# Key sums of the stick-breaking attention: fp32 operands replaced by a high and a low part, split by ScalarE and GpSimd

## The reference

```
z = jnp.einsum('bthd,bhsd->bhts', qb, kh).astype(jnp.float32) * scale
past = s_pos[None, :] < t_pos[:, None]
log_1m = jnp.where(past, jax.nn.log_sigmoid(-z), 0.0)
tail = lax.cumsum(log_1m, axis=3, reverse=True) - log_1m
w = jnp.where(past, jnp.exp(jax.nn.log_sigmoid(z) + tail), 0.0)
return jnp.einsum('bhts,bhsd->bthd', w.astype(v.dtype), vh)
```

## Time and profile before

| | us |
|---|---|
| median of 3 runs (1684.21 to 1684.86) | 1684.85 |
| the profiled execution, its own time | 1684.58 |
| its span, first to last instruction | 1682.5 |
| PE busy | 1669.5 (99%) |
| DVE busy | 1229.0 (73%) |
| ACT busy | 861.7 (51%) |
| POOL busy | 107.3 (6%) |

### The profile page before, as it was taken

How to read it: one execution, slowest core, us unless ns; L and a number is a source line. 1 busy time by engine, 2 the same in 40 slices (tenths; PEclk the granted TensorE clock), 3 DMA queues, 4 the chain that set the end, 5 groups by cost and what they waited for, 6 DMA issues and landing times.

```text
span 1682.5 us, 24105 instructions
## 1 busy us (share of the span) xinstructions
PE 1669.5 (99%) x9040; PEld 1405.3 (84%) x9040; DVE 1229.0 (73%) x1841; ACT 861.7 (51%) x1108; POOL 107.3 (6%) x141
## 2 busy tenths in 40 slices
PE   8999999999999999999999999999999999999999
PEld 6888887788888888878778888888888787788887
DVE  6777847776777676779876767776767798767675
ACT  6444556644445444566564444444445665644442
POOL 2000100200002000101011000030001010100000
PEclk9999999999999999999999999999999999999999
DMA  7645443465547555534444555475554344446552
GB/s 280 230 175 201 152 160 126 163 225 182 192 175 242 197 193 189 166 123 149 128 163 167 219 183 191 175 236 206 190 192 164 121 149 130 163 166 217 186 189 75
DMA packets 69812, 299.95 MB, mean 178 GB/s; under 512 B 5408, under 2 KB 7680, under 8 KB 44512
## 3 DMA queue, kind: packets, MB, share of 16 engines
q1 hardware_dynamic: 66752, 291.52, 49.3%
q0 software_dynamic: 2688, 7.19, 1.6%
q10 hardware_dynamic: 288, 0.10, 0.0%
HBM read 297.74 MB, written 1.05 MB: 178 GB/s over the span
## 4 chain that ended last, share of the span: by engine, by line
PE 98%; DVE 1%; ACT 1%; DMA 0%; issue 0%; POOL 0%; ACTq 0%
PE ps L590 26%; PE ps L601 14%; PE ps L643 9%; PE ps L644 9%; PE ps L645 9%; PE ps L878 6%; PE ps L880 6%; PE ps L879 6%; PE ps L565 2%; PE ps L566 2%; PE ps L968 1%; PE ps L568 1%; PE ps L366 1%; PE ps L572 1%; PE ps L1049 1%; PE ps L1021 1%
## 5 line engine op out<-in xcount | busy, mean ns | idle before, releaser
L273 DVE TENSOR_TENSOR w_lo<-raw,w_hi 128x2048 fp32r<-128x2048 f32 x275 | 627.3, 2293 | 141.6 <-ACT w_hi L266 140.8
L266 ACT ACTIVATE w_hi<-raw 128x2048 fp32r<-128x2048 f32 x275 | 524.2, 1912 | 254.5 <-PE ps L601 166.2
L590 PE MATMUL ps<-aT,w_hi 128*128 128x512 f32 x1920 | 489.9, 392 | 0.0
L590 PEld LDWEIGHTS ps<-aT,w_hi 128*128 128x128 f32 x1920 | 344.2, 188 | 59.5
L601 PEld LDWEIGHTS ps<-aT,w_lo 128*128 128x128 f32 x1920 | 270.4, 190 | 25.1
L601 PE MATMUL ps<-aT,w_lo 128*128 128x256 f32 x1920 | 277.2, 282 | 0.0
L791 DVE TENSOR_REDUCE tmp<-ps 128x256 f32<-128x512 f32 x240 | 164.7, 686 | 131.9 <-PE ps L601 131.7
L643 PE MATMUL ps<-w_hi,act_hi 128*128 128x512 f32 x576 | 226.1, 393 | 0.8 <-ACT gate_or_gain L913 0.8
L644 PE MATMUL ps<-w_lo,act_hi 128*128 128x512 f32 x576 | 224.9, 390 | 0.0
L645 PE MATMUL ps<-w_hi,act_lo 128*128 128x512 f32 x576 | 224.2, 389 | 0.0
L878 PE MATMUL ps<-w_hi,aT 128*128 128x512 f32 (+1 forms) x432 | 171.6, 397 | 0.0
(11 more groups left out here) (303 smaller groups left out, 1561.6 us busy)
## 6 DMA issues: line engine op xcount, KB each, us to landing
raw<-in_ffn_units SPq DMA_DIRECT2D x197, 1024.0 KB, 5.0
raw<-in_w_in SPq DMA_DIRECT2D x34, 1024.0 KB, 5.3
raw<-in_w_gate SPq DMA_DIRECT2D x24, 1024.0 KB, 5.1
raw<-in_w_out SPq DMA_DIRECT2D x12, 1024.0 KB, 4.8
qk_t<-in_nsa_cmp_w POOLq DMA_DIRECT2D x8, 512.0 KB, 5.8
raw<-in_w_br_b SPq DMA_DIRECT2D x4, 1024.0 KB, 4.8
raw<-in_w_br_a SPq DMA_DIRECT2D x2, 1024.0 KB, 4.9
raw<-in_w_br_c SPq DMA_DIRECT2D x2, 1024.0 KB, 4.9
```

The lines of the kernel that those rows point to most:

```text
L266: nc.scalar.activation(w_hi[w][:, :], raw[k][:, :], ACT.Copy).then_inc(hi_ready, 1)
L273: nc.vector.tensor_tensor(w_lo[w][:, :], raw[k][:, :], w_hi[w][:, :].bitcast(F32), ALU.subtract)\
L590: nc.tensor.matmul(gu_bank(like, j), hi[:, k, GU_COLS[j]:GU_COLS[j] + P], aT[:, :, a, :], start=a == 0, stop=a == KC - 1, skip_group_check ...
```

## The change

In both large mixers the sums over the keys take four one-pass products for two plain fp32 products. ScalarE writes `hi`, a copy of the logarithms in type F32R (`act_sb_split`), and GpSimd writes `lo = pt_buf - hi` (`pool_sb_split`). Half 0 goes into the first 768 columns of `oT_hi` and `oT_lo`, half 1 into `act_hi` and `act_lo`. The two constant matrices are copied once in each mixer into the last 256 columns of `oT_lo`, by ScalarE (`sums_neg`). TensorE waits for `sb_sp_lo`, which GpSimd counts, where it waited for `sb_sp_ready`. The two quarters of tile (5, 0) now stand ahead of the two halves of the sums, one each. On VectorE `ahead(9)` moves behind the compressed keys.

```diff
+        def sb_split(half, h):
+            if half == 0:
+                return [o[:, 3 * P * h:3 * P * (h + 1)] for o in oT_flat]
+            return [a[:, 0:3 * P] for a in act_flat[h]]
+        def act_sb_split(act, half, li):
+            act.wait_ge(sem("sb_sp_ready"), 2 * li + half + 1)
+            for h in range(2):
+                last = nc.scalar.activation(sb_split(half, h)[0], sb_view(ptb, half)[:, h, :], ACT.Copy)
+            last.then_inc(sem("sb_sp_hi"), 1)
+        def pool_sb_split(pool, half, li):
+            pool.wait_ge(sem("sb_sp_hi"), 2 * li + half + 1)
+            for h in range(2):
+                hi, lo = sb_split(half, h)
+                last = nc.gpsimd.tensor_tensor(lo, sb_view(ptb, half)[:, h, :], hi.bitcast(F32), ALU.subtract)
+            last.then_inc(sem("sb_sp_lo"), 1)
...
-                add(0, 3 * P, const("tail_neg"), own)
-                add(P, S, const("ones_neg"), own[:, S:3 * P])
+                for own in sb_split(half, h % 2):
+                    add(0, 3 * P, tail, own)
+                for own in sb_split(half, h % 2):
+                    add(P, S, ones, own[:, S:3 * P])
...
                 if i == 0:
+                    for half_ in range(2):
+                        pool_sb_split(pool, half_, ph["mix2_before"])
                     wait(pool, "kc_ss_ready", ph)
...
             for half_ in range(2):
-                pe.wait_ge(sem("sb_sp_ready"), 2 * li + half_ + 1)
+                quarter(5, 0, half_)
+                pe.wait_ge(sem("sb_sp_lo"), 2 * li + half_ + 1)
                 pe_sb_logw(pe, half_, ph)
-            tile(5, 0)
             tile(5, 1)
...
             ahead(7)
+            nc.scalar.activation(sums_neg, consts[:, place["ones_neg"][0]:place["ones_neg"][0] + 2 * P], ACT.Copy)
             evac(3, 0)
...
+            act_sb_split(act, 0, li)
             evac(4, 0)
             ahead(9)
+            act_sb_split(act, 1, li)
             evac(4, 1)
...
                 last.then_inc(sem("sb_sp_ready"), 1)
-            ahead(9)
             wait(dve, "kcvc_ready", ph)
...
+            ahead(9)
             qk_normed(0, qk_first, "qk_first_ready")
```

More of the change, by code:

```diff
@@ L1796, in pe_sb_scores @@
             last.then_inc(ev("sb_z_ready", ph)[0], 1)
+        oT_flat = [o[:, :, :].rearrange("p a b -> p (a b)") for o in (oT_hi, oT_lo)]
+        act_flat = [[a[:, :, :].rearrange("p a b -> p (a b)") for a in pair] for pair in zip(act_hi, act_lo)]
+        sums_neg = oT_flat[1][:, 6 * P:8 * P]
+        def sb_split(half, h):
[13 more added lines that the diff above has]
+            last.then_inc(sem("sb_sp_lo"), 1)
         def pe_sb_logw(pe, half, ph):
-            sp_ = sb_view(ptb, half)
+            tail, ones = sums_neg[:, P:2 * P], sums_neg[:, 0:P]
             for h in (2 * half, 2 * half + 1):
-                dst, own = sb_bank(h), sp_[:, h % 2, :]
+                dst = sb_bank(h)
                 def add(c0, c1, a, b):
                     return nc.tensor.matmul(dst[:, c0:c1], a, b, start=False, stop=True, skip_group_check=True)
-                add(0, 3 * P, const("tail_neg"), own)
-                add(P, S, const("ones_neg"), own[:, S:3 * P])
+                for own in sb_split(half, h % 2):
+                    add(0, 3 * P, tail, own)
+                for own in sb_split(half, h % 2):
+                    add(P, S, ones, own[:, S:3 * P])
                 add(0, P, ident_bf, notpast_bf)
```

## The result

| | us |
|---|---|
| before, median of 16 runs | 1684.40 (1684.13 to 1686.10) |
| after, median of 16 runs | 1688.82 (1686.91 to 1689.20) |
| ratio | 1.0023, 95% interval 1.0016 to 1.0030 |
| the profiled execution after, its own time | 1687.26 |

The change made the kernel 4.4 us slower, 0.26%, just over the 0.2% named as the least that a measurement tells. The runs of after fall into two groups: four from 1686.91 to 1687.48, at a mean granted clock of 0.999, and twelve from 1688.50 to 1689.20, at 0.998 but for one. The profiled execution is one of the four.

A forecast was written before the change was run, and what follows sets the result against it. TensorE, busy 1669.5 of 1682.5 us, bounds the kernel. A mixer saves 1.3 and waits 2.5, +1.2; two mixers +2.4 give 1687.0 for the profiled execution, 1687.2 as median, 8-in-10 range 1681.8 to 1689.8.

The forecast's parts named there:

- The saving: TensorE's sums over the keys: a head takes 0.69 us, saving 1.3 us a mixer, bounds 0.75 and 1.7.
- The port: GpSimd and VectorE instructions with two SBUF operands take turns at a shared port, the waiting engine next; GpSimd's subtraction 1.0 us.
- The wait: TensorE before half 1 of the sums waits for GpSimd's fourth subtraction, 2.5 us a mixer; bounds 2.0 and 3.7.
- Who stands behind: Later users of VectorE: normalization 3.0 us late, 1.6 us slack at the attention's weights; 0.2 at most, left out.
- rival A: Wait at the sums hidden, GpSimd beside VectorE or keeping the port: 1682.2 us, 1681.4 to 1683.4; 22%.
- The clock: Granted clock in idle stretches: a fall would add to rival B; 1.00 in the first 5 us speaks against; unsized.
- rival B: Longer wait at the sums, 3.7 us or more, VectorE also late for the attention: 1689.6 to 1692 us; 14%.
- The moved `ahead(9)`: On VectorE behind the compressed keys: free where its unit is used, but puts 2.29 us of port between GpSimd's instructions.
- rival C: Short wait at the sums, about as long as the saving: 0 to +0.7 us a mixer, 1684.9 to 1686; 12%.
- Rival D: One-pass products of the sums cost as much as fp32 ones for 128 columns: about 1690 us; 2%.

The follow-up runs named there:

- e2: The changed kernel with VectorE's large subtraction ahead(9) held until both low parts of the second half are there: 1688.68 us, ratio 1.0022.
- e8: The changed kernel without the low parts, sums from the high parts alone, not the reference's precision: 1680.17 us, ratio 0.9973.
- e5: The kernel before with only the change's new order, sums in plain fp32 without a split: 1684.55 us, ratio 1.0000.
- e1: The changed kernel with quarter (5, 1, 0) put ahead of TensorE's wait for the second half's low parts: 1685.83 us, ratio 1.0007.
- e4: The changed kernel with the four low parts made by VectorE in place of GpSimd: 1683.46 us, ratio 0.9993.
- e9: The changed kernel with ahead(9) back ahead of the compressed keys and quarter (5, 1, 0) ahead of TensorE's wait: 1683.77 us, ratio 0.9996.
- e3: The changed kernel with 15 unused products of 256 columns on TensorE ahead of its wait for the second half: 1685.99 us, ratio 1.0009.
- e6: The changed kernel with ahead(9) on VectorE left ahead of the compressed keys, as in the kernel before: 1683.72 us, ratio 0.9996.

## Why the prediction came out as it did

The forecast was +2.4 us, 1687.2, with the port as its mechanism. The median is 1688.8: inside the range and inside the forecast's own 1686.0 to 1688.9, by its edge, and over the 1688.2 that I had put as the border to slower, to which I gave 26%. The profiled execution, 1687.26, is 0.3 over the 1687.0 that the sum gave for it. That is luck: its wait was 1.3 us too long over the two mixers, and a fall of the clock for 1.5 us was not in the sum.

- **The saving**: 0.69 us a head forecast. Measured at full clock 1.33 for the two heads of mixer 1's half 0 and 1351.28 - 1349.85 = 1.43 for mixer 2's half 1, together 2.76 for four heads. That it is the forecast to the hundredth is chance, since the two halves differ by 0.10; prices by start distances of like products in the small mixer were enough. The row behind that half 1:

```profile
1351.28 0.36 PE L878 MATMUL ps<-w_hi,aT 128*128 128x256 f32 x1
```

- **The port**: the turns held as I had them from the earlier trace rows; e2 shows them by taking them away (1.98 and 2.29 us), e8 by taking GpSimd's subtractions away (0.76 for the masks). That the engine which waits always comes next did not hold in general (the last section has e5).
- **The wait**: 2.5 forecast; 1.70 measured as idle time and 1.86 from start to start, which is how the forecast counts. Both are below the lower bound of 2.0. Two terms were mis-sized. The first is the start of GpSimd's third instruction, 755.65 in my order. The trace after runs 0.26 us ahead of that before (tile (4, 1) ends at 752.89 for 753.15), so this means 755.39 there, and it came at 754.97, 0.4 early. I let the masks end at 754.55, which means 754.29; both were over by 751.64 + 2.28 = 753.92, so ScalarE, GpSimd's third and VectorE's subtraction all came some 0.4 earlier. The second is the length of the turns: from the third's start to the fourth's end I had 759.9 - 755.65 = 4.25 us, and the pair took 4.01. Together that is the 0.6. The order of turns that I had worked out for the second half, third, subtraction, fourth, is what the subtraction's 2.88 us and the end of the pair at 758.98 fit. GpSimd's price of 1.0 us was right: 1.98 for two in e2.
- **Who stands behind**: nothing at the attention, as said: from the products with v to its first transposes it is 20.86 us after and 783.97 - 763.12 = 20.85 before in mixer 1, and 21.05 against 20.86 in mixer 2, without a wait. But I had let one customer on TensorE out: the transpose of the compressed keys, which wait behind the normalization on VectorE. In the changed kernel TensorE's own lateness covers it; when the wait at the sums is covered or taken away it costs 0.6 to 2.0 us a mixer (e1, e2, e4, e9). So rival A, the hidden wait, could not have given 1682.2 by covering the wait alone.
- **The clock**: the term that I had put at nothing, and the largest error of the forecast. I wrote of a fall only under rival B and set against it that the clock stands at 1.00 in the kernel's first 5 us, where TensorE is mostly idle. As I read the rows below, that stretch was a false witness. The first products of 512 columns behind it, in the timeline of TensorE after:

```profile
10.46 0.63 PE L566 MATMUL ps<-w_lo,aT 128*128 128x512 f32 x1
10.88 0.63 PE L565 MATMUL ps<-w_hi,aT 128*128 128x512 f32 x1
11.31 0.63 PE L566 MATMUL ps<-w_lo,aT 128*128 128x512 f32 x1
...
14.31 0.39 PE L566 MATMUL ps<-w_lo,aT 128*128 128x512 f32 x1
14.54 0.39 PE L565 MATMUL ps<-w_hi,aT 128*128 128x512 f32 x1
```

And the windows of the same two stretches, with the columns as above:

```profile
9.90:11.50 1.60, 1.60 (x6) 1.14 (x4) 1.60 (x3) 1.60 (x3) 0.00 (x0) 1.00 1.04 440
```

```profile
14.00:16.00 2.00, 2.00 (x11) 1.65 (x10) 1.51 (x1) 2.00 (x4) 0.89 (x2) 1.00 0.97 406
```

The products start 0.42 to 0.43 apart at first and 0.23 apart 3 us later, and the windows give 1.00 for both. Behind the fall in mixer 1, 256 columns took 0.21 to 0.22, which is half of the 0.43. So I infer that the engine was at the lower clock there and that the column doesn't show it; no run tests this. The kernel before has the same 0.42 to 0.43 between 10.56 and 11.41. Read so, the start of the kernel was evidence for rival B's condition. The clock fell behind a wait of 1.7 us in mixer 1 of the profiled execution, and the fall cost nearly as much as the wait itself. A mixer costs 0.65 us without it and 1.53 more with it: with two falls that makes 2 x 0.65 + 2 x 1.53 = 4.4 us, as the medians differ; with one it is 2.8, and the profiled executions differ by 2.7. e3 confirms the term by keeping TensorE busy: -2.8 us.
- **The moved `ahead(9)`**: I had said that it puts 2.29 us of the port between GpSimd's instructions, and so much is right, but I had costed it only as a part of the wait. e6 prices it: 1.0 us of wait a mixer and with that the clock, 5.1 us in all, more than the change costs. With it left where it was, the time would have been 1683.7, below even rival C.
- **Rival D**: 0.06 us for a 128-column product, and 0.11 where the next weights are late: refuted.

What stays open: why the same idle time lowers the clock in one mixer and leaves it in the other. No run here separates the two.

## What to carry to other kernels

When work is handed to GpSimd to spare TensorE, look first at which of VectorE's instructions read two operands from SBUF in that stretch, and in which order the two engines will issue: here one such instruction in front of GpSimd's pair instead of within it was worth 5 us, some 3 of them by the clock. A wait of TensorE costs more than its length if the clock falls behind it, as it did here in most runs with waits of 1.7 and 2.0 us, so such a wait that can't be removed is worth covering with any work. And a covered wait is only gone if the engine that was late is not late for the next customer: follow its queue to all of them.

## What the runs showed of the hardware that was not expected

TensorE's granted clock went from 1.00 to 0.64 and 0.54 in the two stretches behind an idle time of 1.70 us, and the work of these 4.2 us took 1.5 us longer than the same work in mixer 2. By the run times, which are the only sign in runs without a trace, this came in about 28 of the 32 mixers of 16 runs. It was not sure to come: 1.71 us in mixer 2 of that execution, and 2.01 and 2.03 us in the profiled execution of e2, left the clock at 1.00. The mean clock stayed at 1.000 in all eleven runs each of e1, e6 and e4, with waits of up to 1.1, 0.7 and 0.6 us. At the kernel's start the clock column reads 1.00 while products of 512 columns stand 0.42 us apart for 0.23 later; the distance of like products is worth reading beside the column. The turns on the port also reach very small instructions: GpSimd's root over 30 x 1 values takes 1.51 us beside VectorE's product in the changed kernel and 0.53 in e2:

```profile
758.94 1.51 POOL L1890 TENSOR_TENSOR small<-small,stats 30x1 f32<-30x1 f32 x1
```

```profile
757.55 0.53 POOL L1890 TENSOR_TENSOR small<-small,stats 30x1 f32<-30x1 f32 x1
```

Nor does the engine that waits always come next. In e5 the same root is issued at 754.19, beside VectorE's subtraction, which is over at 756.3, and it also lets VectorE's next product pass:

```profile
754.19 3.65 POOL L1865 TENSOR_TENSOR small<-small,stats 30x1 f32<-30x1 f32 x1 [4.43 <-DVE small L2320]
```

```profile
756.24 1.21 DVE L2232 TENSOR_TENSOR tmp<-proj,small 128x1024 f32<-128x1024 f32 x1
```

In e8 it stands beside the same two instructions, takes 2.61 us and is done before the product is. What decides the turn, no run here shows.
